# First out-projection: the sample search's sixteen rounds shared 3,3,3,2,2,2,1,0 over the eight chunks, loop written out

## The chip, the cores and the metric

The kernel runs on one core of one Trainium2 chip. The metric is the device time of one launch in microseconds; lower is better. The core's engines work side by side and meet at semaphores: TensorE (PE in the profile; its weight loads PEld), VectorE (DVE), ScalarE (ACT), GpSimd (POOL) and SyncE (SP), which starts the loads of weights.

## The reference

One inference step of a two-layer decoder trunk, for a prompt of 1024 positions and a sample batch of 8 x 8 positions, in float32, model width 1024. Layer 0 has sparse attention beside a pooling mixer and one output projection over both. Layer 1 has a spatial gating unit. Each layer does

    x = x + rmsnorm(mixer(rmsnorm(x)))
    x = x + rmsnorm(swiglu(rmsnorm(x)))

In the sparse attention an indexer scores all keys for each query, and only the best take part:

    score = where(kpos <= qpos, score, -inf)
    _, sel = top_k(score, topk)

For the sample batch topk is 130: (512 + 8) // 4 keys out of 520 for each of 64 queries.

## The kernel before

**Halves and phases.** The work is done in two halves, g = 0 (512 prompt positions) and g = 1 (512 positions and the 64 of the sample batch). Both halves' input projections and indexer scores come first. Then, for each half in turn: attention, the out-projection ("out"), a post-norm with residual and pre-norm, the feed-forward in two halves (gate/up, down), layer 1's gating unit with its own out-projection ("oo"), a norm, and the second feed-forward.

**An out-projection** has eight chunks of 128 output features. A chunk is 24 matmuls of 128x512 on TensorE (line 714): each float32 product is split into three passes with the tiles w_hi and w_lo. For each chunk ScalarE makes w_hi of a later chunk (L1335), squares the chunk's result out of PSUM into one of two buffers (L1663) and copies it to SBUF (L1664). GpSimd makes w_lo, the difference of the raw and the rounded weights (L1856, "the pass" below). VectorE adds the squares to a running sum (L2024, `add_square`), for the first seven chunks; the eighth chunk's squares go to TensorE by themselves. ScalarE's squares of chunk n wait for the addition of chunk n-2.

**The norm behind it.** TensorE sums over the partitions by matmuls with a column of ones: it opens (L817), adds the running sum (after the seventh addition) and the last squares (L822), closes (L827), and runs filler matmuls (L832, `hold`) between and behind. ScalarE takes the square root (L1368), VectorE the reciprocal (L2037, `inverse`), TensorE spreads it over the partitions (L848, `spread`), and VectorE, ScalarE and GpSimd work through the residual, the next norm's squares and the split into two parts (L2498, L2500, L1710, L1711, L1888). TensorE starts the next stage's first matmuls on the parts as they come (L748). The same sequence stands behind every out-projection and feed-forward.

**The sample search.** The best 130 of the 584 columns of `SCS` (64 rows: the queries) are found in rounds of eight: MAX8 (L2105) writes the eight largest, MATCH_VALUE_LOAD and MATCH_REPLACE8 (L2112) mark them. `top_round` is one MAX8 and one marking. Sixteen rounds find 128, and a closing MAX8 (L2647), a memset that leaves two of the eight, and a MATCH_REPLACE8 (L2651) find the last two. All of this stands on VectorE in the first half's out-projection: `sample_rounds` puts two rounds behind each of the first six additions and four behind the seventh; the closing three and the reciprocal follow in program order. The first six additions and their rounds run in a hardware loop of three turns (`dve.Fori`). Inside it the semaphore values are read from a register, and the helper `wait` puts a nop behind such a wait. The result of the search is used in the second half's attention. The search over the prompt's scores (`big`) starts in the feed-forward that follows. Layer 1's out-projection for the same half has the same eight chunks and the same norm, with no rounds on VectorE.

Of the kernel before, what the change touches and what calls it, by code (L numbers as in the profile page):

```python
# [35 lines left out]
NB = D // P  # L36
# [121 lines left out]
def wait(eng, sem, value):  # L158


    if isinstance(value, int):
        if value > 0:
            eng.wait_ge(sem, value)
        return
    eng.wait_ge(sem, value)
    eng.nop(nofuse=True)


def build_kernel(nc, ins, outs):
# [3 lines left out]
    def phase(name, g, layer=0, half=0):  # L173
        return by[name, g, layer, half]

    with ExitStack() as ctx:
# [3 lines left out]
        def place(name, shape, dt, at=None):  # L180

            size = 2 if dt == BF16 else 4
            n = size * int(np.prod(shape[1:]))
            if at is None:
                at = cursor[0]
                cursor[0] = (at + n + 31) // 32 * 32
                assert cursor[0] <= nc.sbuf_usable_end, (name, cursor[0], nc.sbuf_usable_end)
            return nc.alloc_sbuf_tensor_at(name, shape, dt, offset=at), at
# [6 lines left out]
        WR, _ = place("w_raw", [P, 2, FH * P], F32)  # L195
        WH, _ = place("w_hi", [P, 2, FH * P], F32R)
        WL, _ = place("w_lo", [P, 2, FH * P], F32R)
        KT, kt_at = place("keys_t", [P, SEQ + NS], F32)
        IKT, _ = place("idx_keys_t", [P, SEQ + NS], F32)
        VN, _ = place("values", [P, 9, P], F32)  # L200
        IW, _ = place("idx_weights", [P, 9, 8], F32)
# [4 lines left out]
        SS, _ = place("square_sums", [P, 5 * P], F32)  # L206
        RT, _ = place("root_rstd", [P, 2, 5], F32)
        CT, _ = place("constants", [P, NKEEP], F32)
        GC, _ = place("gains", [P, 84], F32)
        IDB, _ = place("ident_bf16", [P, P], BF16)  # L210
        MCB, _ = place("causal_bf16", [P, P], BF16)
        EB, _ = place("spread_bf16", [NS, DB, NS], BF16)
        IWT, _ = place("idx_weights_t", [8, NS], F32)
        M8, _ = place("top8", [P, 5, 8], F32)
        MX, _ = place("row_stats", [P, 4, 16], F32)
        PGT, _ = place("pages", [1, DB * NPG], I32)
        T16, _ = place("first_windows", [P, 16], F32)
        ZERO, _ = place("zero_columns", [P, 16], F32)
# [87 lines left out]
        def S(name):  # L306
            if name not in sems:
                sems[name] = ctx.enter_context(nc.semaphore(name))
            return sems[name]
# [45 lines left out]
        def norm_at(kind, g, s):  # L355
            if kind == "load":
                return g
            return 2 + 4 * g + s
# [7 lines left out]
        def z_at(g, s):  # L366
            return 1 + 4 * g + s
# [15 lines left out]
        SCS = SB[0:NS, SS_AT:SS_AT + KCOL + 8]  # L383
# [6 lines left out]
        SMALL = LOW + TOPK_P // 8  # L390
# [1625 lines left out]
        def _(dve):  # L2016
            def sum_zero(z):
                dve.memset(SS[:], 0.0).then_inc(S("ss_zero"), 1)

            def add_square(mp, n, p, g, z):  # L2020
                wait(dve, S("sq_p"), 8 * mp + n + 1)
                wait(dve, S("ss_p"), 7 * mp + n)
                dve.wait_ge(S("ss_zero"), z + 1)
                dve.tensor_tensor(SS[:, 0:T[g]], SS[:, 0:T[g]], SQ[:, p, 0:T[g]], ALU.add).then_inc(S("ss_p"), 1)  # L2024
# [76 lines left out]
            def top_max(spans, r):  # L2101

                wait(dve, S("top"), 2 * r)
                for m, s in spans:
                    ins_ = dve.max(M8[0:s.shape[0], m, :], s)  # L2105
                ins_.then_inc(S("top"), 1)

            def top_mark(spans, r):

                wait(dve, S("top"), 2 * r + 1)  # L2110
                for m, s in spans:
                    ins_ = dve.match_replace(out=s, in_to_replace=M8[0:s.shape[0], m, :], in_values=s, imm_value=CHOSEN)  # L2112
                ins_.then_inc(S("top"), 1)

            def top_round(spans, r):
                top_max(spans, r)
                top_mark(spans, r)
# [268 lines left out]
            def attend_sample():  # L2386
                dve.wait_ge(S("qk_mm"), 64)
                dve.memset(QZ[:], 0.0).then_inc(S("qz0"), 1)
                dve.tensor_scalar(MKS[:], SCS[:, 0:KCOL], SPLITTER, MASK, ALU.is_gt, ALU.mult).then_inc(S("mks"), 1)
                for b in range(DB):  # L2390
                    dve.wait_ge(S("qks_mm"), b + 1)
                    dve.tensor_reduce(MX[0:NS, 0, b:b + 1], PSF[0:NS, 1024 * (b % 2):1024 * (b % 2) + KCOL], AX.X, ALU.max).then_inc(S("mxs"), 1)
                    dve.wait_ge(S("mxs"), b + 1)
                    dve.tensor_scalar(MX[0:NS, 1, b:b + 1], MX[0:NS, 0, b:b + 1], -(HD ** -0.5), None, ALU.mult).then_inc(S("nms"), 1)
                    dve.wait_ge(S("exps"), b + 1)
                    dve.reciprocal(MX[0:NS, 3, b:b + 1], MX[0:NS, 2, b:b + 1]).then_inc(S("invs"), 1)
                    dve.wait_ge(S("invs"), b + 1)
                    pr = PRS[:, b % 2, :]
                    dve.tensor_scalar(pr, pr, MX[0:NS, 3, b:b + 1], None, ALU.mult).then_inc(S("ps_norm"), 1)
                dve.wait_ge(S("osc_hi"), 1)  # L2400
                for half in range(2):
                    r = slice(64 * half, 64 * half + 64)
                    for j in range(4):
                        at = AR[r, 0, j, 512:T[1]].rearrange("p (b t) -> p b t", b=DB)
                        lo = AR[r, 1, j, 512:T[1]].rearrange("p (b t) -> p b t", b=DB)
                        ins_ = dve.tensor_tensor(lo, PS[r, 7, :].rearrange("p (b h t) -> p h b t", b=DB, h=8)[:, 4 * half + j],
                                                 at.bitcast(F32), ALU.subtract)
                ins_.then_inc(S("osc"), 1)

            def out_like(ph, g, s, extra=None):  # L2410
                mp = norm_at("post", g, s)
                z = z_at(g, SZ[s])
                sum_zero(z)
                with dve.Fori(0, ph.iters - 1) as i:
                    for p in (0, 1):
                        add_square(mp, 2 * i + p, p, g, z)
                        if extra:
                            extra(i, p)
                add_square(mp, NB - 2, 0, g, z)
                if extra:  # L2420
                    extra(ph.iters - 1, 0)
                    extra(ph.iters - 1, 1)

            big = [(m, score(m + 4)) for m in range(4)]
            BIG0 = SMALL + 17
# [210 lines left out]
            for g in range(2):  # L2636
                attend(g)
                if g:
                    attend_sample()
                if g == 0:  # L2640
                    def sample_rounds(i, p):
                        for q in range(2):
                            top_round([(4, SCS)], SMALL + 4 * i + 2 * p + q)
                    out_like(phase("out", 0), 0, 0, sample_rounds)

                    dve.wait_ge(S("top"), 2 * (SMALL + 16))
                    dve.max(M8[0:NS, 4, :], SCS).then_inc(S("top"), 1)  # L2647
                    dve.wait_ge(S("top"), 2 * (SMALL + 16) + 1)
                    dve.memset(M8[0:NS, 4, TOPK_S % 8:8], DUMMY).then_inc(S("m8_cut"), 1)
                    dve.wait_ge(S("m8_cut"), 1)  # L2650
                    dve.match_replace(out=SCS, in_to_replace=M8[0:NS, 4, :], in_values=SCS, imm_value=CHOSEN).then_inc(S("top"), 1)  # L2651
                else:
                    out_like(phase("out", 1), 1, 0)
                post(g, 0)
                at = BIG0
                for layer in range(2):
                    for half in range(2):
                        run = g == 0 and layer == 0
                        gate_up(phase("gu", g, layer, half), at if run else None)
                        at += FH  # L2660
                        down(phase("dn", g, layer, half), 1 + 2 * layer, at if run else None)
                        at += 4
                    if layer == 0:
                        post(g, 1)
                        gate(g)
                        out_like(phase("oo", g), g, 2)
                        post(g, 2)
                    else:
                        post(g, 3)
# [32 lines left out]
```

## Time and profile before

| | |
|---|---|
| median of 3 runs | 2754.19 us (2754.17 to 2757.58) |
| profiled execution | 2752.42 us, its span 2750.2 us |
| TensorE | busy 94% of the span |
| VectorE, ScalarE, GpSimd | busy 47%, 37%, 44% |
| mean granted clock of TensorE | 0.969 of 2.4 GHz |
| matmuls of L714 | 65% of the chain of waits |
| DMA | 83 GB/s over the span |

The span runs from the first to the last instruction of one execution seen by the hardware profiler; all times in rows are microseconds from its start unless marked ns. A timeline row names start, duration, engine, line, operation, written tile <- read tiles, shapes (partitions x elements), and a count where like instructions are merged. Square brackets give the engine's idle time ahead and what ended it. The granted clock is TensorE's, as a share of 2.4 GHz (0.50 is 1.2 GHz).

### The profile page before, as it was taken

To read this page: it belongs to the slowest core of one execution; us is meant where nothing else is said; L and a number is where in the kernel's file an instruction comes from. 1 tells how busy PE (TensorE), PEld (TensorE's weight loads), DVE (VectorE), ACT (ScalarE), POOL (GpSimd) and SP (SyncE) were. 2 spreads that over 40 slices of the span, in tenths; PEclk is the share of its full clock that TensorE was granted. 3 is DMA by queue.
4 is the path that set the end of the run, shared out by engine and by line. 5 is a ranking of instruction groups with operands and counts; after the bars stand their busy time and mean duration, and the time that the engine had idled before them with its cause. 6 is when DMAs were issued, how large, how long until landed. Compare 5 with 4: busy or idle time off the path is not lost.

```text
span 2750.2 us, 43876 instructions
## 1 busy us (share of the span) xinstructions
PE 2594.5 (94%) x15403; PEld 2312.8 (84%) x15407; DVE 1285.0 (47%) x1779; ACT 1028.9 (37%) x1516; POOL 1212.7 (44%) x608
## 2 busy tenths in 40 slices
PE   6979859999999999999978899999999999999999
PEld 4769547788887787888867599999999999999999
DVE  4467777796887454303456433211234253220234
ACT  4545743432324434323246434222224435222222
POOL 4444243554554335545545224444444334443442
PEclk9989879999999999999989999999999999999999
DMA  6445011233332222333331211232232221232232
GB/s 163 115 103 145 16 58 54 69 100 91 99 101 72 87 82 71 101 91 99 101 109 35 85 55 54 84 92 70 83 89 73 76 72 49 83 91 73 81 90 75
DMA packets 447742, 229.45 MB, mean 83 GB/s; under 512 B 86460, under 2 KB 439440, under 8 KB 447127
## 3 DMA queue, kind: packets, MB, share of 16 engines
q1 hardware_dynamic: 447647, 228.21, 29.1%
q8 instruction: 56, 0.92, 0.1%
q14 instruction: 39, 0.32, 0.0%
HBM read 212.84 MB, written 15.43 MB: 83 GB/s over the span
## 4 chain that ended last, share of the span: by engine, by line
PE 77%; DVE 6%; ACT 3%; issue 2%; POOL 1%; DVEq 0%; POOLq 0%; ACTq 0%
PE psum L714 65%; PE psum L748 2%; PE psum L822 1%; PE psum L992 1%; PE psum L1084 1%; PE psum L1069 1%; DVE probs_t L2374 1%; DVE scores L2112 1%; DVE top L2105 1%; PE psum L1092 1%; DVE row_stats L2365 1%; PE psum L848 1%; PE psum L1194 1%; ACT act_split L1710 0%; PE psum L1141 0%
## 5 line engine op out<-in xcount | busy, mean ns | idle before, releaser
L1856 POOL TENSOR_TENSOR w_lo<-w_raw,w_hi 128x1024 fp32r<-128x1024 f32 (+1 forms) x334 | 854.6, 2559 | 1248.0 <-ACT w_hi L1335 1247.9
L714 PE MATMUL psum<-act_split,w_hi 128*128 128x288 f32 (+1 forms) x6096 | 1344.1, 329 | 11.4 <-POOL w_lo L1856 4.9
L714 PEld LDWEIGHTS psum<-act_split,w_hi 128*128 128x128 f32 x6096 | 980.7, 189 | 97.7 <-issue 5.9
L1335 ACT ACTIVATE w_hi<-w_raw 128x1024 fp32r<-128x1024 f32 (+1 forms) x334 | 375.0, 1124 | 1288.2 <-PE psum L714 1263.4
L714 PE MATMUL psum<-act_split,w_lo 128*128 128x288 f32 (+1 forms) x3048 | 832.4, 328 | 0.0
L714 PEld LDWEIGHTS psum<-act_split,w_lo 128*128 128x128 f32 x3048 | 519.6, 189 | 39.7
L714 PE MATMUL psum<-hidden_split,w_hi 128*128 128x288 f32 (+1 forms) x2112 | 461.8, 327 | 0.0
L714 PEld LDWEIGHTS psum<-hidden_split,w_hi 128*128 128x128 f32 x2112 | 339.5, 189 | 27.3
L714 PE MATMUL psum<-hidden_split,w_lo 128*128 128x288 f32 (+1 forms) x1056 | 287.9, 327 | 0.0
L2433 DVE TENSOR_TENSOR temps<-psum,root_of_input 128x512 f32<-128x512 f32 (+1 forms) x88 | 63.4, 721 | 358.2 <-PE psum L714 343.5
L2439 DVE TENSOR_TENSOR temps<-psum,temps 128x512 f32<-128x512 f32 (+1 forms) x88 | 63.3, 719 | 357.4 <-PE psum L714 332.4
L2441 DVE TENSOR_TENSOR hidden_split<-temps,hidden_split 128x512 f32 (+1 forms) x88 | 171.3, 1947 | 92.9 <-ACT hidden_split L1675 92.9
L2024 DVE TENSOR_TENSOR square_sums<-square_sums,squares 128x512 f32<-128x512 f32 (+1 forms) x63 | 144.6, 2295 | 126.1 <-ACT squares L1663 88.5
L714 PEld LDWEIGHTS psum<-hidden_split,w_lo 128*128 128x128 f32 x1056 | 179.6, 189 | 13.7
L2112 DVE MATCH_REPLACE8 scores<-top,scores 128x640 f32<-128x640 f32 (+3 forms) x192 | 169.8, 890 | 0.0
L2105 DVE MAX8 top<-scores 128x8 f32<-128x640 f32 (+3 forms) x192 | 164.5, 897 | 2.2
L1875 POOL TENSOR_TENSOR temps<-temps,root_of_input 128x512 f32<-128x512 f32 (+1 forms) x88 | 119.9, 1362 | 25.4 <-ACT temps L1672 25.4
L1888 POOL TENSOR_TENSOR act_split<-mixed,act_split 128x512 fp32r<-128x512 f32 (+1 forms) x48 | 65.5, 1365 | 66.6 <-ACT mixed L1711 66.6
L748 PE MATMUL psum<-act_split,w_hi 128*128 128x288 f32 (+1 forms) x288 | 73.1, 357 | 7.1 <-POOL act_split L1888 5.1
L1092 PE MATMUL psum<-probs_t,values_split 128*128 128x512 f32 x216 | 68.3, 428 | 10.7 <-DVE probs_t L2374 10.6
L1672 ACT ACTIVATE temps<-temps 128x512 f32<-128x512 f32 (+1 forms) x88 | 56.7, 645 | 47.7 <-DVE temps L2433 47.7
L1069 PE MATMUL psum<-keys_split,queries_split 128*128 128x384 f32 (+5 forms) x192 | 60.2, 431 | 14.7 <-ACT probs_short L1582 8.3
(296 smaller groups left out, 2327.6 us busy)
## 6 DMA issues: line engine op xcount, KB each, us to landing
w_raw<-in_w_ffn_gate_up SPq DMA_DIRECT2D x352, 256.0 KB, 3.1
w_raw<-in_w_ffn_down SPq DMA_DIRECT2D x64, 384.0 KB, 3.7
w_raw<-in_w_ffn_down SPq DMA_DIRECT2D x64, 320.0 KB, 4.1
w_raw<-in_w_in_odd SPq DMA_DIRECT2D x64, 256.0 KB, 3.0
w_raw<-in_w_in_even SPq DMA_DIRECT2D x60, 256.0 KB, 3.9
w_raw<-in_w_out_odd SPq DMA_DIRECT2D x32, 256.0 KB, 3.0
x_rows<-in_x_prompt SPq DMA_DIRECT2D x8, 512.0 KB, 6.1
w_raw<-in_w_out_even SPq DMA_DIRECT2D x32, 128.0 KB, 2.8
```

Source lines behind the costliest of these rows:

```text
L714: mm = pe.matmul(PS[:, 2 * p + b, 0:hi - lo], w[:, p, at], x(k)[:, lo:hi], start=(k == 0 and w is WH and x is x_hi), stop=(k == ph.kt - 1 ...
L748: mm = pe.matmul(PS[:, 2 * p + b, 0:hi - lo], w[:, p, at], x(k)[:, lo:hi], start=(k == 0 and w is WH and x is a_hi), stop=(k == ph.kt - 1 ...
L1069: mm = pe.matmul(PS[:, 2 * x + b, 0:w], QST[:, h, :], KS[:, h // 4, part, b * w:b * w + w], start=t < 2 and part == 0, stop=t >= 2 and par ...
L1092: mm = pe.matmul(PS[:, 6 + z, :], VS[:, v, kk, :], PT[:, kc % 2, q, :], start=kk == 0 and v == 0 and q == 0, stop=kk == t and v == 1)
L1335: act.activation(WH[:, p, 0:n], WR[:, p, 0:n], ACT.Copy).then_inc(S("w_hi"), 1)
L1856: pool.tensor_tensor(WL[:, p, 0:n], WR[:, p, 0:n], WH[:, p, 0:n].bitcast(F32), ALU.subtract).then_inc(S("w_lo"), 1)
L1875: pool.tensor_tensor(TT[:, 0, 0:T[g]], TT[:, 0, 0:T[g]], RB[:, 0:T[g]], ALU.mult).then_inc(S("gated"), 1)
L1888: pool.tensor_tensor(AR[:, 1, n, 0:T[g]], src, AR[:, 0, n, 0:T[g]].bitcast(F32), ALU.subtract).then_inc(S("a_lo"), 1)
L2024: dve.tensor_tensor(SS[:, 0:T[g]], SS[:, 0:T[g]], SQ[:, p, 0:T[g]], ALU.add).then_inc(S("ss_p"), 1)
L2105: ins_ = dve.max(M8[0:s.shape[0], m, :], s)
L2112: ins_ = dve.match_replace(out=s, in_to_replace=M8[0:s.shape[0], m, :], in_values=s, imm_value=CHOSEN)
L2441: dve.tensor_tensor(flat(HR[:, 1, ds(i, 1), 0:T[g]]), TT[:, 1, 0:T[g]], flat(HR[:, 0, ds(i, 1), 0:T[g]].bitcast(F32)), ALU.subtract).then_ ...
```

## The change

`out_like` on VectorE no longer takes a callback that places two rounds per addition, but a list of eight numbers. With a list the loop is written out: seven additions at fixed semaphore values, and behind chunk n as many rounds as the list says. The first half's out-projection of layer 0 gets (3, 3, 3, 2, 2, 2, 1, 0). Before it was 2 behind each of the first six additions and 4 behind the seventh. The other out-projections keep the loop. No other engine's program changes.

```diff
-            def out_like(ph, g, s, extra=None):
+            def out_like(ph, g, s, rounds=None):
                 mp = norm_at("post", g, s)
                 z = z_at(g, SZ[s])
                 sum_zero(z)
+                if rounds:
+                    r = SMALL
+                    for n in range(NB):
+                        if n < NB - 1:
+                            add_square(mp, n, n % 2, g, z)
+                        for _ in range(rounds[n]):
+                            top_round([(4, SCS)], r)
+                            r += 1
+                    assert r == SMALL + 16
+                    return
                 with dve.Fori(0, ph.iters - 1) as i:
                     for p in (0, 1):
                         add_square(mp, 2 * i + p, p, g, z)
-                        if extra:
-                            extra(i, p)
                 add_square(mp, NB - 2, 0, g, z)
-                if extra:
-                    extra(ph.iters - 1, 0)
-                    extra(ph.iters - 1, 1)
...
                 if g == 0:
-                    def sample_rounds(i, p):
-                        for q in range(2):
-                            top_round([(4, SCS)], SMALL + 4 * i + 2 * p + q)
-                    out_like(phase("out", 0), 0, 0, sample_rounds)
+                    out_like(phase("out", 0), 0, 0, (3, 3, 3, 2, 2, 2, 1, 0))
```

## Rows read from the trace of the kernel before

**Rows 1.** The page's head: span, and busy time, share and instructions of each engine.

```profile
span 2750.2 us, 43876 instructions
PE 2594.5 (94%) x15403; PEld 2312.8 (84%) x15407; DVE 1285.0 (47%) x1779; ACT 1028.9 (37%) x1516; POOL 1212.7 (44%) x608
```

**Rows 2.** Chain of waits, 370:520: start us, us, engine, what, line.

```profile
482.58 0.74 DVE scores L2651
483.32 0.10 DVE root_rstd L2037
483.46 2.09 PE psum L848 x8
```

**Rows 3.** Timeline of TensorE, 476:509: start us, us, engine, line, op, tiles, count.

```profile
476.23 0.29 PE L817 MATMUL psum<-zero_columns,constants 128*128 128x10 f32 x2
...
479.25 1.74 PE L832 MATMUL psum<-constants 128*128 128x256 f32 x4
...
503.10 1.03 PE L822 MATMUL psum<-constants,temps 128*128 128x1 f32 x8
...
508.36 0.73 PE L714 MATMUL psum<-act_split,w_hi 128*128 128x512 f32 x2 [1.37 <-POOL w_lo L1856]
```

**Rows 4.** Timeline of ScalarE, squares of chunks 1 and 3, square root.

```profile
444.87 0.58 ACT L1663 ACTIVATE squares<-psum 128x512 f32<-128x512 f32 x1
...
455.75 0.58 ACT L1663 ACTIVATE squares<-psum 128x512 f32<-128x512 f32 x1
...
479.77 0.17 ACT L1368 ACTIVATE root_rstd<-psum 128x4 f32<-128x4 f32 x1
```

**Rows 5.** Timeline of VectorE through the eight chunks.

```profile
440.49 2.20 DVE L2024 TENSOR_TENSOR square_sums<-square_sums,squares 128x512 f32<-128x512 f32 x1 [7.21 <-ACT squares L1663]
442.61 0.75 DVE L2105 MAX8 top<-scores 64x8 f32<-64x584 f32 x1
...
445.33 0.74 DVE L2112 MATCH_REPLACE8 scores<-top,scores 64x584 f32<-64x584 f32 x1
446.00 2.05 DVE L2024 TENSOR_TENSOR square_sums<-square_sums,squares 128x512 f32<-128x512 f32 x1
...
474.99 0.75 DVE L2105 MAX8 top<-scores 64x8 f32<-64x584 f32 x1
...
476.63 0.76 DVE L2105 MAX8 top<-scores 64x8 f32<-64x584 f32 x1
...
483.25 0.16 DVE L2037 RECIPROCAL root_rstd<-root_rstd 128x4 f32<-128x4 f32 x1
```

**Rows 6.** Timeline of GpSimd: the passes of chunks 0 and 1.

```profile
439.75 2.40 POOL L1856 TENSOR_TENSOR w_lo<-w_raw,w_hi 128x1024 fp32r<-128x1024 f32 x1 [15.70 <-ACT w_hi L1335]
445.11 2.39 POOL L1856 TENSOR_TENSOR w_lo<-w_raw,w_hi 128x1024 fp32r<-128x1024 f32 x1 [2.96 <-ACT w_hi L1335]
```

**Rows 7.** The additions' line over the span: ns min/median/max, starts, forms.

```profile
L2024 DVE TENSOR_TENSOR square_sums<-square_sums,squares x63: 691/2374/3182, 13.4 to 2729.0; 128x512 f32<-128x512 f32 x35, 128x576 f32<-128x576 f32 x28
```

**Rows 8.** Timeline of TensorE and VectorE around the twin, layer 1, same half.

```profile
1030.20 0.29 PE L817 MATMUL psum<-zero_columns,constants 128*128 128x10 f32 x2
...
1034.18 1.16 PE L848 MATMUL psum<-constants,root_rstd 128*128 128x128 f32 x8
...
1058.03 0.74 PE L714 MATMUL psum<-act_split,w_hi 128*128 128x512 f32 x2 [1.37 <-POOL w_lo L1856]
...
1033.95 0.18 DVE L2037 RECIPROCAL root_rstd<-root_rstd 128x4 f32<-128x4 f32 x1 [4.91 <-ACT root_rstd L1368]
```

**Rows 9.** Stretches: us; busy us (xcount) of the five engines; granted clock; DMA share; GB/s.

```profile
479.50:480.00 0.50, 0.50 (x3) 0.38 (x3) 0.47 (x2) 0.43 (x2) 0.42 (x1) 0.58 0.00 0
483.50:484.00 0.50, 0.50 (x2) 0.50 (x3) 0.00 (x0) 0.00 (x0) 0.00 (x0) 0.50 0.00 0
```

**Rows 10.** Timeline of TensorE, the norm behind the first feed-forward.

```profile
885.25 1.38 PE L822 MATMUL psum<-constants,temps 128*128 128x1 f32 x8
...
892.46 0.79 PE L714 MATMUL psum<-act_split,w_hi 128*128 128x512 f32 x2 [0.49 <-DVE mixed L2518]
```

## The prediction

> **What bounds the kernel now.** I read the page first: TensorE is busy for 94% of the span [rows 1], so time can be won only where TensorE stands still or runs at its lower clock. Next the chain of waits around the first out-projection. Ahead of the spread of the norm's factors (L848) it runs through no matmul but through the sample search's last MATCH_REPLACE8 and the reciprocal behind it on VectorE [rows 2]. The timelines give the times. The eight chunks' matmuls end at 476.23, where the closing of the sum of squares starts (L817); the spread starts 7.23 us later, at 483.46 [rows 2, 3], and the next stage's matmuls at 508.36 [rows 3]. ScalarE has the square root ready at 479.77 + 0.17 = 479.94 [rows 4], the reciprocal on VectorE is issued at 483.25 [rows 5]. So the norm waits 3.31 us for VectorE, which still works through the rounds placed behind its last addition.
>
> **Where VectorE's time goes in the eight chunks.** TensorE delivers a chunk each 5.44 us (the squares of chunk 1 start at 444.87, those of chunk 3 at 455.75 [rows 4]). An addition (L2024) of the first chunk takes 2.20 us though the shortest of the 63 takes 0.69 [rows 5, 7]: it ends at 442.69, 0.54 us behind GpSimd's w_lo pass (439.75 + 2.40 = 442.15 [rows 6]). It waits for the pass and then runs. The Trainium skill (SBUF — State Buffer, section "SBUF: two separate sides") has the rule: a port pair is an exclusive lock between a GpSimd operation and a VectorE operation with two SBUF inputs, and whoever comes first keeps it for its whole instruction. The trace agrees (2.20 against 0.69 us). The rule also speaks against the change, since an addition that starts just ahead of a pass would hold the pass; by my times below none does.
>
> **The change, step by step.** The work stays: seven additions, sixteen rounds, the closing MAX8, memset and MATCH_REPLACE8. Two things change.
>
> (a) The loop is written out. A round in written-out code, as behind the last addition now, takes 476.63 − 474.99 = 1.64 us [rows 5]; I take it for all sixteen. In the loop two rounds and an addition fill the distance between chunks anyway, so this by itself gives nothing. More code to fetch costs 0 if it is fetched ahead; the upper end is the slack found in (b), behind which each us costs one.
>
> (b) The rounds go from 2,2,2,2,2,2,4 behind the seven additions to 3,3,3,2,2,2,1; the eighth chunk has neither addition nor rounds. VectorE's course, from rows:
> Addition 0 ends as now, the rounds start at 442.61 [rows 5]. Three rounds (4.92) go to 447.53. The pass of chunk 1 is over by then (445.11 + 2.39 = 447.50 [rows 6]), so addition 1 costs 0.69 in place of the 2.05 of now (446.00 [rows 5]) and ends at 448.22. Three rounds to 453.1, addition 2 to 453.8 (passes follow each 5.44 us, so that of chunk 2 is over at about 452.9), three rounds to 458.7, addition 3 (pass over at about 458.4) to 459.4, two rounds to 462.7.
> The squares of chunk 4 are ready at about 461.8, and here VectorE is early again. Addition 4 meets the pass of chunk 4, over at 463.8 or 463.9, and ends 0.54 later at 464.4. Two rounds to 467.7; addition 5 meets its pass and ends at about 469.8; two rounds to 473.1. Addition 6 waits for its pass as now, and the next instruction starts at 474.99, as now [rows 5].
> Then one round in place of four: 476.63. The closing three take what they take now: the reciprocal at 483.25 less 474.99 less four rounds (6.56) is 1.70, so VectorE is free at 478.33, 1.6 us ahead of the square root's end.
> Is a chunk late on the way? ScalarE squares chunk n only after addition n−2, since two buffers take turns. Squares of chunk 3 start at 455.75 [rows 4] and need addition 1, over at 448.2: 7.5 us to spare. For chunk 5 they start near 466.6 and need addition 3 (459.4): 7.2. The sum over the blocks needs addition 6, which doesn't move. So TensorE's chunks stay where they are, and no queue of SP or GpSimd is moved past; VectorE issues no DMA here.
>
> **What is late next.** The reciprocal follows the root. In the kernel's twin of this stretch, the second layer's out-projection for the same half, VectorE has only additions: closing of the sum at 1030.20, reciprocal at 1033.95, 3.75 us later [rows 8]. Here that is 476.23 + 3.75 = 479.98, 3.27 us earlier than now. From there the spread, the residual and the split are one chain on TensorE, VectorE, ScalarE and GpSimd, and move with it. The price of the spread depends on TensorE's clock.
> Upper end: at full clock all goes as in the twin: 1058.03 − 1030.20 = 27.83 us from the closing to the next stage's first matmul [rows 8]. Here it takes 508.36 − 476.23 = 32.13 [rows 3]. The difference is 4.30: 3.27 of the wait, and about 0.9 because the eight matmuls of the spread took 2.09 us at 1.2 GHz [rows 2, 9] and in the twin 1.16 [rows 8].
> Lower end: the granted clock fell from 2.4 to 1.2 GHz between 479.50 and 480.00 (mean 0.58 [rows 9]), while TensorE still ran the four filler matmuls issued at 479.25 for 1.74 us [rows 3], so ahead of its idle time. If that fall stays, the fillers end at 480.99 and the spread starts there and not at 480.2: 483.46 − 480.99 = 2.47 us gained, at an unchanged low clock.
> The same instructions in the twin kept the full clock, so the fall is not the sequence's alone. The Trainium skill (TensorE: Matmul & The Clock Gate, "Part 1: The HAM clock gate") says that the monitor runs free of the kernel's start, so one program can meet it differently in each execution; by that both ends occur. No single trace can show it. From the two stretches, one of each kind, I take the middle of 2.47 and 4.30, rounded: **3.5 us**. The profiled execution took 2752.42 us (span 2750.2 and 2.2 around it) and would take 2748.9; it lies 1.8 below the median of the three runs, from which the same 3.5 leaves 2754.19 − 3.5 = **2750.7 us**, own range 2749.9 to 2751.7.
>
> **The rivals.**
> A, the clock later helps further. All behind this stretch moves forward by some 3 us and meets the clock's changes elsewhere. The norms ahead of a stage show a price: from the last sums (L822 on temps) to the first big matmul it takes 508.36 − 503.10 = 5.26 us at full clock and 892.46 − 885.25 = 7.21 at the low one [rows 3, 10]: 1.95. One more such norm that keeps the clock gives 5.45, 2748.7; two give 7.4, 2746.8. For it: the low clock at 885 struck in the middle of TensorE's work (eight sums in 1.38 us, at 503 in 1.03), so it hangs on where the norm lies. Against: nothing says which way it goes.
> B, the slower side by the clock: norms that kept the clock, as the one at 503, lose it. It decides from two of them on: 2 × 1.95 = 3.9 is more than 3.5 and gives 2754.6; three give 2756.5.
> C, the slower side by VectorE: in the new order more rounds run beside GpSimd's passes (in chunks 1 to 3 nearly whole passes). Were MAX8 and MATCH_REPLACE8 held as the addition is, VectorE would have 5.44 − 2.40 = 3.04 us a chunk. Its work from 442.15 on is sixteen rounds of 1.64, six additions of 0.69 and the closing 1.70, together 32.1 us; seven gaps take 21.3, the remaining 10.8 starts when the last pass is over, at about 480, and ends near 491: 7.5 later than now, 2761.7. It decides from 483.25 − 478.33 = 4.9 us of holding in all. Against it: the MATCH_REPLACE8 at 445.33 took 0.74 us beside the pass of 445.11 to 447.50 [rows 5, 6], as long as the one that closes the search at 482.58, when no pass runs [rows 2].
> D, the gain is hidden: code fetch or a late addition 6 keeps the reciprocal near 482.5, up to 0.8 gained: 2753.6. Against: VectorE runs such straight code behind the loop with rounds 1.64 apart, in the loop two take 446.00 − 442.61 = 3.39 [rows 5].
>
> **How the numbers follow.** Chances: forecast 0.69, A 0.14 (most of it past one norm), B 0.10, C 0.02, D 0.05. About 0.2% (5.5 us) is what a measurement of this kernel can tell from no change, so the forecast itself lies within it. Faster by over 0.2% (below 2748.7) is A, less its cases at the edge, and a little of the forecast where runs scatter: 0.13. Slower by over 0.2% (above 2759.7) is C and a tail of B: 0.03. The rest, 0.84, is no difference. The range takes in one helping and one and a half losing norms and the scatter between executions (2754.17 to 2757.58 before): 2747.0 to 2754.8.
>
> **What would show it right or wrong.** In the profile after: additions 1 to 3 at about 0.7 us, additions 4 to 6 still stretched to the pass's end; one round behind addition 6; the closing MATCH_REPLACE8 over by 478.5 and VectorE idle ahead of the reciprocal, released by ScalarE's root; the spread 4.0 us (full clock) or 4.8 us (low) behind the closing of the sum and not 7.2; from closing to the next stage's first matmul 27.8 to 29.7 us. It is wrong if a round beside the pass takes more than 1.7 us, if ScalarE's squares wait for an addition, or if the stretch shrinks and the total doesn't follow; then the clock at the later norms must show where it went.

## The result: slower, and the profile after

The changed kernel takes 2769.82 us (median of 20 runs, 2738.74 to 2776.2) against 2754.46 (20 runs, 2741.97 to 2770.78). The ratio is 1.0036, with a 95% interval of 1.0019 to 1.0052 (such intervals stand in square brackets below). It is taken over all runs and is smaller than the ratio of the two medians, 1.0056, since the runs of the changed kernel spread widely. So the change is slower, where 3.5 us faster was forecast, too little to tell from no change; and the median lies outside the range of 2747.0 to 2754.8. The medians are 15.4 us apart, the means 9.4. The median alone hides what happened: the changed kernel's runs lie in two groups (a lower and an upper one, in the words used below), five between 2738.74 and 2750.7, fifteen between 2764.32 and 2776.2. The profiled execution, 2738.74 us with a span of 2736.5, is of the lower group, so it shows what the change does where it was made, but not where the time went.

The page's head of the kernel after [rows 1 of before]:

```profile
span 2736.5 us, 43807 instructions
PE 2583.3 (94%) x15407; PEld 2300.7 (84%) x15407; DVE 1279.7 (47%) x1779; ACT 1029.0 (38%) x1516; POOL 1212.7 (44%) x608
```

The timeline of TensorE in the kernel after, columns as in [rows 3] ("the closing" below is the start of the first L817, as in the prediction):

```profile
475.76 0.29 PE L817 MATMUL psum<-zero_columns,constants 128*128 128x10 f32 x2
...
478.78 1.11 PE L832 MATMUL psum<-constants 128*128 128x256 f32 x4
479.75 1.16 PE L848 MATMUL psum<-constants,root_rstd 128*128 128x128 f32 x8
...
500.89 1.91 PE L848 MATMUL psum<-constants,root_rstd 128*128 128x128 f32 x8
...
504.63 0.73 PE L714 MATMUL psum<-act_split,w_hi 128*128 128x512 f32 x2 [0.72 <-DVE temps L2438]
```

The spread (first L848) starts 479.75 − 475.76 = 3.99 us behind the closing, in place of 7.23, and takes 1.16 us in place of 2.09 [rows 2, 3]. The next stage's matmuls start 504.63 − 475.76 = 28.87 us behind it, in place of 32.13: 3.26 us gained.

The timeline of VectorE in the kernel after [rows 5 of before]; lines left out are the rounds and the other additions:

```profile
446.98 0.67 DVE L2024 TENSOR_TENSOR square_sums<-square_sums,squares 128x512 f32<-128x512 f32 x1
...
461.64 2.33 DVE L2024 TENSOR_TENSOR square_sums<-square_sums,squares 128x512 f32<-128x512 f32 x1
...
474.52 0.75 DVE L2105 MAX8 top<-scores 64x8 f32<-64x584 f32 x1
...
477.16 0.74 DVE L2653 MATCH_REPLACE8 scores<-top,scores 64x584 f32<-64x584 f32 x1
479.51 0.18 DVE L2037 RECIPROCAL root_rstd<-root_rstd 128x4 f32<-128x4 f32 x1 [1.61 <-ACT root_rstd L1368]
```

The second to fourth additions (446.98 is the second) take 0.67 or 0.68 us and the last three 2.14 to 2.33; the search is over at 477.90, and the reciprocal now waits 1.61 us for ScalarE's root.

The stretch in which the clock fell before [rows 9], in the kernel after, same columns:

```profile
479.50:480.00 0.50, 0.50 (x4) 0.26 (x3) 0.18 (x1) 0.00 (x0) 0.00 (x0) 1.00 0.00 0
```

### The profile page after: what moved, and what is told of

It is laid out like the page before. It is cut to its first block, busy times and chain, and to the rows that moved or that the text cites. A ratio compares the mean times of both kernels' runs of the same rounds, so it can differ in the third digit from the quotient of the medians.

```text
span 2736.5 us, 43807 instructions
## 1 busy us (share of the span) xinstructions
PE 2583.3 (94%) x15407; PEld 2300.7 (84%) x15407; DVE 1279.7 (47%) x1779; ACT 1029.0 (38%) x1516; POOL 1212.7 (44%) x608
## 4 chain that ended last, share of the span: by engine, by line
PE 79%; DVE 5%; ACT 3%; issue 1%; POOL 1%; DVEq 0%; POOLq 0%; ACTq 0%
PE psum L714 67%; PE psum L748 2%; PE psum L822 2%; PE psum L992 1%; PE psum L1084 1%; PE psum L1069 1%; DVE probs_t L2374 1%; PE psum L1092 1%; PE psum L848 1%; DVE row_stats L2365 1%; PE psum L1194 1%; DVE scores L2112 0%; ACT act_split L1710 0%; PE psum L1141 0%; PE psum L832 0%
## 5 line engine op out<-in xcount | busy, mean ns | idle before, releaser
L2024 DVE TENSOR_TENSOR square_sums<-square_sums,squares 128x512 f32<-128x512 f32 (+1 forms) x63 | 140.4, 2229 | 126.5 <-ACT squares L1663 88.9
L714 PEld LDWEIGHTS psum<-hidden_split,w_lo 128*128 128x128 f32 x1056 | 178.7, 188 | 13.7
```

The lines of the kernel that those rows point to most:

```text
L714: mm = pe.matmul(PS[:, 2 * p + b, 0:hi - lo], w[:, p, at], x(k)[:, lo:hi], start=(k == 0 and w is WH and x is x_hi), stop=(k == ph.kt - 1 ...
```

## The experiments

Each was timed beside the kernel before, whose medians in the four sets of runs were 2754.61, 2755.41, 2755.68 and 2754.68 (29, 35, 22 and 17 runs). The reading that came out of them is this; what of it is only inferred stands at the end of the next section. The written-out code moves the code behind it on VectorE. A stall of some 0.4 us, for which the profile names no other engine, moves with it and falls into the second half's first long tile of attention, at about 1435 us, onto the chain of waits. After that, TensorE meets its clock otherwise: in most executions its granted clock stays at 1.2 GHz through the whole of the following sample attention, which costs 18 to 20 us in one piece.

**1. The change again, unaltered, to profile an execution of the upper group.**

> The changed kernel once more, unaltered. Its executions so far lie in two groups, five between 2738 and 2751 us and fifteen between 2764 and 2776, the second with a mean granted clock of TensorE of about 0.960 in place of 0.969. Theory 1 (TensorE): the loss is extra time at 1.2 GHz or slower matmul issue in a later stage, far from the changed lines; the closing-to-next-stage stretch stays 28 to 30 us in every execution and a profile in the upper group shows some 50 us more at low clock elsewhere. Theory 2 (VectorE): the upper group has a late VectorE in the changed out-projection or in the gate/up loop behind it; then the stretch 476 to 857 us is longer by 15 us or more.

Measured: 2764.13 us (2750.5 to 2775.48, 12 runs), ratio 1.0029 [1.0007, 1.0052]. The profiled execution took 2773.13 (span 2770.9). Its out-projection is the one shown above: spread 480.20 − 476.22 = 3.98 us behind the closing. The loss is elsewhere. From the L817 at about 1405 us to the next one is 241.4 us in the kernel before, 240.8 after, and 260.0 here. TensorE's timeline, first the kernel before, then this run:

```profile
1406.35 0.29 PE L817 MATMUL psum<-zero_columns,constants 128*128 128x10 f32 x2
...
1647.75 0.28 PE L817 MATMUL psum<-zero_columns,constants 128*128 128x10 f32 x2
```

```profile
1404.84 0.29 PE L817 MATMUL psum<-zero_columns,constants 128*128 128x10 f32 x2
...
1664.82 0.28 PE L817 MATMUL psum<-zero_columns,constants 128*128 128x10 f32 x2
```

That stretch holds the second half's attention, the sample attention (eight batches of small matmuls, lines L1108 to L1141) and the out-projection. The sample attention begins at 1551.88 in the kernel before, and the out-projection's first matmul comes at 1594.32; here it is 1548.4 and 1611.00. Stretches of 20 us from its start, columns as in [rows 9]; the kernel before:

```profile
1546.30:1566.30 20.00, 15.74 (x68) 8.04 (x67) 7.31 (x16) 8.18 (x22) 0.00 (x0) 0.83 0.21 60
1566.30:1586.30 20.00, 19.95 (x128) 12.59 (x126) 7.80 (x20) 8.98 (x27) 0.00 (x0) 1.00 0.64 185
1586.30:1606.30 20.00, 16.31 (x99) 15.81 (x100) 3.50 (x12) 4.31 (x16) 1.76 (x1) 0.74 0.00 1
```

The same stretches in the profiled execution of the change run again:

```profile
1544.80:1564.80 20.00, 16.82 (x50) 7.98 (x51) 6.34 (x14) 7.06 (x20) 0.00 (x0) 0.59 0.21 60
1564.80:1584.80 20.00, 20.00 (x70) 11.59 (x70) 3.79 (x11) 5.73 (x15) 0.00 (x0) 0.50 0.60 178
1584.80:1604.80 20.00, 19.33 (x76) 13.41 (x76) 4.68 (x12) 4.54 (x13) 0.00 (x0) 0.50 0.00 0
```

TensorE is as busy (20.00 of 20.00 us), but at a granted clock of 0.50 it issues 70 matmuls where it issued 128. In the kernel before it is at 1.2 GHz from 1554.8 to 1561.6 and from 1588.9 to 1599.2 only, here from 1548.4 to 1616.7. The matmuls show it one by one. The same line in the same batch, first after (lower group), then the change run again, from the timelines of TensorE:

```profile
1560.17 1.07 PE L1141 MATMUL psum<-page_keys_t,queries_sample 128*64 128x512 f32 x2
```

```profile
1561.28 1.97 PE L1141 MATMUL psum<-page_keys_t,queries_sample 128*64 128x512 f32 x2
```

**2. Written out, but with the rounds where they were.** In the changed kernel:

```diff
-out_like(phase("out", 0), 0, 0, (3, 3, 3, 2, 2, 2, 1, 0))
+out_like(phase("out", 0), 0, 0, (2, 2, 2, 2, 2, 2, 4, 0))
```

> Loop written out, rounds as before (2,2,2,2,2,2,4). Theory A (code): the written-out code shifts VectorE's later code and thereby its loops; then this kernel loses as the change does, median near 2770 us. Theory B (time): the earlier norm moves the later stages to where TensorE's clock gate hits them worse; then this kernel, whose norm is not earlier (reciprocal near 483), stays with the kernel before, about 2754 us.

Measured: 2775.3 us (2752.11 to 2778.85, 12 runs), ratio 1.0071 [1.0053, 1.0089]. Clock at 1.2 GHz from 1554.4 to 1622.7. Eleven of the twelve runs are of the upper group. So the loss isn't caused by the norm that comes earlier: without that gain it is larger. The written-out code alone brings it.

**3. The gain in the loop's form.** Four rounds ahead of the first addition, two behind each of the first six, as the loop has them, none behind the last. In the kernel before:

```diff
             def sample_rounds(i, p):
                 for q in range(2):
-                    top_round([(4, SCS)], SMALL + 4 * i + 2 * p + q)
+                    top_round([(4, SCS)], SMALL + 4 + 4 * i + 2 * p + q)
+            for q in range(4):
+                top_round([(4, SCS)], SMALL + q)
             out_like(phase("out", 0), 0, 0, sample_rounds)
...
                 add_square(mp, NB - 2, 0, g, z)
-                if extra:
-                    extra(ph.iters - 1, 0)
-                    extra(ph.iters - 1, 1)
```

> Loop kept with two rounds behind each addition, the last four rounds moved ahead of the first addition, where VectorE waits 7.2 us for the first squares (four rounds take 6.6). Theory A (code): no loss, and the 3.3 us of the wait are gained: about 2750.5 us. Theory B (time): the norm is as early as in the change, so it loses likewise: median near 2770 us.

Measured: 2751.58 us (2747.84 to 2759.22, 12 runs), ratio 0.9987 [0.9973, 1.0001]; run again at the end of this section, 2750.6. From VectorE's timeline of the profiled execution:

```profile
478.84 0.18 DVE L2037 RECIPROCAL root_rstd<-root_rstd 128x4 f32<-128x4 f32 x1 [3.24 <-ACT root_rstd L1368]
```

The search is over 3.24 us ahead of the root. The four rounds cost nothing ahead of the first addition, since VectorE waited 7.21 us there for the first chunk [rows 5] and still waits 0.73 us; and no upper group appears (12 runs here, 12 more below).

**4 and 5. Moving the code without the change, and the change with its code moved further.** One-column memsets on a tile that nobody reads at that time, ahead of the first addition, where VectorE waits anyway: six in the kernel before, nineteen in the changed kernel.

```diff
                 sum_zero(z)
+                if g == 0 and s == 0:
+                    for k in range(6):          # 19 in the changed kernel
+                        dve.memset(T16[64 * (k & 1):64 * (k & 1) + 64, k // 2:k // 2 + 1], 0.0)
```

> The kernel before with six one-column memsets ahead of the first addition, where VectorE is idle: its later code stands six instructions further on, nothing else moves. Theory A1 (place of the code): the 0.37 us stall in front of the fourth normalisation of the second half's first long tile (L2337 before) appears as in the written-out kernels, the sample attention's matmuls mostly run at 1.2 GHz throughout, median about 2772 us. Rival A2 (the written-out code itself does it, not where later code stands): no stall there, median 2754 us.

Measured: 2754.26 us (2745.19 to 2765.96, 12 runs), ratio 0.9988 [0.9972, 1.0003]: nothing. As it was written, the expectation of theory A1 failed: no stall shows at the fourth L2337. My reading is that six was one too few, and that the stall lies one instruction later, where VectorE waits for ScalarE anyway:

```profile
1438.80 0.69 DVE L2374 TENSOR_TENSOR probs_t<-psum,probs_t 128x512 fp32r<-128x512 f32 x1 [1.85 <-ACT probs_t L1606]
```

This wait is 1.85 us in the kernel before too, so the profile can't show a stall within it; what supports the reading is experiment 8. Elsewhere six memsets do move something: the addition (L2024) at 1000.14 waits 3.40 us in place of 3.01, and the one at 1001.24 with seven memsets 3.38. So a longer wait at that place is not what costs the 20 us.

> The changed kernel with nineteen such memsets (about 1.2 us of idle time): the place where the stall falls moves ahead to an instruction that waits 5.2 us for TensorE anyway. Theory A1: the stall is hidden, the sample attention is mostly at full clock again, the 3 to 4 us of the earlier norm show: median about 2751 us. Rival A2: stays near 2770 us.

Measured: 2752.78 us (2742.53 to 2764.99, 12 runs), ratio 0.9984 [0.9963, 1.0004]. With the code moved further, the changed kernel is no longer slower. Its profile shows no stall at the fourth L2337. Yet four of its twelve runs lie near 2764, the profiled one among them: its clock is at 1.2 GHz from 1550.2 to 1584.3 and again from 1594.6 to 1608.2, and the stretch from L817 to L817 takes 251.0 us, half of the loss. So the low clock can come, for a shorter time, without that stall.

**6 and 7. Is the clock the price?** Filler matmuls on TensorE (`hold`), in the 1.5 and 2.4 us that it is idle at the start of the sample attention, in the changed kernel; then the same in the kernel of experiment 3.

```diff
+                pe.wait_ge(S("exp"), 64)
+                hold(5)
...
+                    if b == 0:
+                        hold(9)
```

> The changed kernel with 5 + 9 filler matmuls on TensorE in its two idle times (1.5 and 2.4 us) at the start of the sample attention. Theory C (the loss is the clock alone: TensorE enters the eight sample batches at 1.2 GHz and their matmuls do not bring it back): the low stretch of some 69 us is gone in most executions, the upper group disappears, median below 2750 us, perhaps 2742. Rival: the sample attention falls to 1.2 GHz whatever runs ahead of it; median stays at 2770, with up to 1 us added.

Measured: 2754.07 us (2748.01 to 2761.22, 12 runs), ratio 0.9991 [0.9976, 1.0005]. The upper group is gone (no run above 2761.22), with the stall where it was. The gain that the expectation also held possible, a median below 2750, did not come. The stretches as above:

```profile
1546.90:1566.90 20.00, 19.25 (x101) 12.72 (x99) 7.62 (x17) 9.22 (x26) 0.00 (x0) 1.00 0.21 60
1566.90:1586.90 20.00, 19.33 (x123) 12.49 (x123) 7.81 (x21) 8.27 (x24) 0.00 (x0) 1.00 0.63 184
```

> The loop kept, four rounds ahead of the first addition, and the same fillers. Theory C: the two low stretches of 7 and 10 us in the sample attention, which cost about half their length, shrink too: 2742 to 2748 us, faster than the kernel before by 6 us or more. Rival: fillers change nothing in executions that recover anyway: 2751.6 us as without them.

Measured: 2753.15 us (2747.18 to 2754.95, 12 runs), ratio 0.9989 [0.9975, 1.0003]. In its profiled execution, the fastest of the twelve (2747.18 us), the stretch from L817 to L817 is 238.4 us in place of 241.1 in experiment 3, as the first fall of the clock in the sample attention is gone; but the median is no lower than the 2751.58 and 2750.6 without fillers, and the 2742 to 2748 of theory C failed. Where the clock recovers by itself, no gain from fillers shows in the total.

**8. One more memset.** The kernel before with seven in place of six.

```diff
-                    for k in range(6):
+                    for k in range(7):
```

> The kernel before with seven one-column memsets ahead of the first addition. With six, the stalls of 0.4 us stood one instruction later than in the written-out kernels, among them at an instruction that waits 1.9 us anyway. With seven they should stand exactly where the change has them, the one ahead of the fourth L2337 included. Theory A1 (place of the code alone): most executions in the upper group, median about 2772 us. Rival A2 (it takes the written-out code): no upper group beyond the share that the kernel before has, median 2754 us.

Measured: 2774.97 us (2773.46 to 2782.08, 11 runs), ratio 1.0066 [1.0045, 1.0086]. All eleven runs are of the upper group. The seventh write of one column, in a place where VectorE waits, costs some 20 us: six gave 2754.26. VectorE's timeline at the fourth normalisation (L2337) of the first long tile, in the kernel before:

```profile
1436.11 0.15 DVE L2332 RECIPROCAL row_stats<-row_stats 128x1 f32<-128x1 f32 x1
1436.30 0.55 DVE L2337 TENSOR_SCALAR probs_long_a<-probs_long_a,row_stats 128x640 f32<-128x640 f32 x1
```

The same with six memsets:

```profile
1436.20 0.15 DVE L2332 RECIPROCAL row_stats<-row_stats 128x1 f32<-128x1 f32 x1
1436.39 0.55 DVE L2337 TENSOR_SCALAR probs_long_a<-probs_long_a,row_stats 128x640 f32<-128x640 f32 x1
```

The same with seven:

```profile
1437.18 0.15 DVE L2332 RECIPROCAL row_stats<-row_stats 128x1 f32<-128x1 f32 x1
1437.75 0.55 DVE L2337 TENSOR_SCALAR probs_long_a<-probs_long_a,row_stats 128x640 f32<-128x640 f32 x1 [0.41 <-DVE row_stats L2332]
```

From start to start it is 0.57 us in place of 0.19. The changed kernel has the same pair, run again 1434.65 − 1434.08 = 0.57 us apart. Of the twelve profiled executions, all five with the written-out loop and no memsets, or with seven memsets, have this pair of 0.57 us (after, experiments 1, 2, 6 and 8); the other seven don't. The chain of waits carries it. Columns: start us, us, what; first the kernel before, then the one with seven:

```profile
1433.55 3.41 issue
1436.96 1.08 PE psum L1084 x4
```

```profile
1434.62 3.79 issue
1438.40 1.09 PE psum L1084 x4
```

TensorE stands still for 3.79 us in place of 3.41. And 130 us later the stretch of sample attention with seven is

```profile
1567.50:1587.50 20.00, 20.00 (x73) 12.43 (x72) 4.68 (x12) 5.73 (x15) 0.00 (x0) 0.50 0.63 184
```

**9. The delay there, with no code moved ahead of it.** In the kernel before, directly ahead of that L2337:

```diff
+                        if hh == 35:
+                            for k in range(6):
+                                dve.memset(T16[64 * (k & 1):64 * (k & 1) + 64, k // 2:k // 2 + 1], 0.0)
```

> The kernel before with six one-column memsets (together about 0.37 us) on VectorE directly ahead of the fourth L2337; all code up to there stays where it was. If the 0.37 us at this point are what sends the sample attention to 1.2 GHz, the median is about 2770 us. If it is another of the moved stalls (at 1000 or 1894 us), 2754 us.

Measured: 2781.28 us (2753.81 to 2783.61, 12 runs), ratio 1.0072 [1.0047, 1.0096]. VectorE's timeline:

```profile
1438.11 0.15 DVE L2332 RECIPROCAL row_stats<-row_stats 128x1 f32<-128x1 f32 x1
1438.21 0.57 DVE L2336 MEMSET first_windows<- 64x1 f32 x6
1438.79 0.55 DVE L2340 TENSOR_SCALAR probs_long_a<-probs_long_a,row_stats 128x640 f32<-128x640 f32 x1
```

From reciprocal to normalisation it is 0.68 us here (L2340 is before's L2337), and the sample attention runs at a granted clock of 0.50 from 1553.2 to 1621.4. So a delay at this point is enough. The six memsets also move the code behind them by six instructions, but so do those of experiment 4, which lost nothing. The median is 11 us above the forecast of about 2770. In the profiled execution 19.6 us of the 30.3 by which its span exceeds that of the kernel before lie in the stretch from L817 to L817; the rest is spread over other stages and was not traced.

**10. The version that beats both, again.**

> The loop kept with four rounds ahead of the first addition, unaltered, to bound its gain: if the 3.0 us of its first timing are the earlier norm, about 2751.6 us again, three to four below the kernel before; if they were scatter, 2754.5.

Measured: 2750.6 us (2748.26 to 2754.11, 12 runs), ratio 0.9982 [0.9971, 0.9992]. It is 4.1 us below the kernel before in the same set of runs. The changed kernel's two medians, of other sets, were 2769.82 and 2764.13. TensorE's timeline:

```profile
478.76 0.29 PE L817 MATMUL psum<-zero_columns,constants 128*128 128x10 f32 x2
...
482.75 1.16 PE L848 MATMUL psum<-constants,root_rstd 128*128 128x128 f32 x8
```

The spread starts 3.99 us behind the closing and at the full clock, as in the changed kernel.

## Why the prediction was wrong

**Step (b) held.** Step (b) is the new order of the rounds. Forecast were one round behind the last addition, the first stretched additions at about 0.7 us, the last three stretched, the search over by 478.5, and a reciprocal released by the root 3.75 us behind the closing: 475.76 and 479.51 are 3.75 apart. The next stage starts 28.87 us behind the closing (27.8 to 29.7 forecast). Of the 4.30 us set as the upper end 3.26 came, because the granted clock stayed full at the first spread but fell at the next norm, where L848 took 1.91 us. The prediction had its lower end from a low clock at the first spread; that 3.26 lies so near its 3.5 is in part luck. Experiment 3, whose form puts no stall at the fourth L2337, shows in the total what an earlier norm is worth: 3.0 us below the kernel before in the first set (its interval still touches no change), 4.1 in the second, where it is clear of it.

**The rule on the port.** The prediction took from the Trainium skill (SBUF — State Buffer, "SBUF: two separate sides") that the port pair is an exclusive lock between a GpSimd operation and a VectorE operation with two SBUF inputs. The trace agrees: in the kernel after, the additions that start in the last 0.13 us of a pass take 0.67 or 0.68 us, those that start in its first microsecond 2.14 to 2.33 (passes of 2.40 us from 444.63, 450.15, 455.51 and from 461.03, 466.40, 471.65). Rival C, which had the rounds held too, fell: in the kernel after, the MAX8 at 450.87 and the MATCH_REPLACE8 at 451.75 run beside the pass that starts at 450.15 and take 0.76 and 0.74 us, those at 453.02 and 453.88, beside no pass, 0.75 and 0.74.

**Step (a) failed.** It said of the written-out code that "this by itself gives nothing", and of the larger code that it "costs 0 if it is fetched ahead; the upper end is the slack found in (b)". Both were sought in the changed stretch, and there it does cost nothing. The step that failed is this term set at nothing with the slack of (b) as its upper end: the length of the code is passed on to all that VectorE runs later, and 950 us behind the change it puts a stall of 0.38 us in front of a normalisation that TensorE waits for. Experiment 2 (written-out code alone: +20.7 us), experiment 8 (no code of the change, only the place moved: +19.3 us) and experiment 5 (the change, its code moved further: −2.6 us) tell place from content. Experiment 9 shows that 0.49 us at the place where the stall lands are enough (0.68 us in place of 0.19).

**The size.** Rivals A and B priced a changed clock at 1.95 us for each norm. The clock was the right resource and the norms the wrong place: 68 us at 1.2 GHz around the sample attention, in place of two falls of 6.8 and 10.3 us, cost 260.0 − 241.4 = 18.6 us in one go. In experiment 6 filler matmuls in TensorE's two waits ahead of it remove this. Rival D (code fetch) had a related cause, but in the changed stretch and capped by the slack there. A rival "the code's place moves a stall onto the chain elsewhere" was missing, and so the chance of slower (0.03) was far too small. The kernel before, too, has some such runs without the change: 7 of its 35 in one set lie between 2766.08 and 2769.02. None of them was profiled, so whether their clock is low in the same place is not known.

**What stays open.** That the 0.4 us stall is a fetch of instructions is an inference: it comes and goes with the count of instructions ahead of it (six against seven), and no record names it. Between the stall at 1436 us and the clock at 1550 lie steps that were seen and not tested. All four profiled executions of the upper group (experiments 1, 2, 8 and 9), and that of experiment 5, lack a fall of the clock for 3.4 us at about 1460 us that the other seven have, and reach the sample attention early: its first L1141 comes 149.53 us behind the L817 at about 1406 in the kernel before, 148.47 with seven memsets. Two profiled executions have the stall and escape: that of after (148.82) and that of experiment 6, which has the fillers. The stall is not sufficient: alone or as a delay it gave over 2762 us in 33 of 35 runs (experiments 2, 8 and 9), together with the earlier norm in 22 of 32 (the changed kernel's two sets). What decides whether the clock returns was not found.

## What to carry to other kernels

Writing out a loop can be an edit to everything that the engine runs later, not to the loop alone; where the same order of work can be had within the loop's form (here four rounds ahead of it), take that. When a gain is seen in its stretch and not in the total, compare the two traces by the distance between repeated marks (here L817 to L817) in executions of either group, and try a few idle instructions as padding before blaming the edit's content. In a stage of small matmuls that starts with short waits, fillers there are worth a try, if some of its executions stay at 1.2 GHz.

## What the runs showed of the hardware that was not expected

VectorE stalls for some 0.4 us, with no other engine as releaser, at a place that depends on how much code stands ahead of it; seven one-column memsets in place of six decided some 20 us. TensorE's clock in the sample attention has two courses in the changed kernel: back to 2.4 GHz after 6.8 us, or 1.2 GHz for 68 us, though TensorE is busy for 20.00 of the 20.00 us of a stretch in it. And at a full granted clock TensorE doesn't always run equally fast. In the second half's first feed-forward, stretches of 100 us, columns as in [rows 9], before and then after:

```profile
1750.00:1850.00 100.00, 100.00 (x752) 100.00 (x751) 20.84 (x16) 25.11 (x28) 45.06 (x20) 1.00 0.30 87
```

```profile
1750.00:1850.00 100.00, 100.00 (x771) 100.00 (x770) 18.73 (x14) 25.50 (x29) 46.01 (x20) 1.00 0.31 89
```

It issues 752 or 771 matmuls. The stage from L817 to L817 around it is 428.4 and 418.1 us long, and in none of the ten other profiled executions under 426.5. So most of the 13.7 us by which the profiled execution of after is the shorter one come from there. Its cause is open, and it is no effect of the change that these runs show.
